# A hybrid decoder step: one key block of prompt attention turned later, and the input projection's row scaling moved from VectorE to ScalarE

## The reference

```python
hn = rms_norm(x, norm_mix)            # x * rsqrt(mean(x*x) + eps) * w
q_down, kv_down, qkv, z, b_raw, a_raw, gm, gg = jnp.split(hn @ w_in, IN_SPLITS, axis=-1)
```

```python
s = (einsum('bqhn,bkhn->bhqk', qn, k_nope) + einsum('bqhr,bkr->bhqk', qr, k_rope)) * MLA_SCALE
p = jax.nn.softmax(jnp.where(key_pos <= q_pos, s, NEG_BIG), axis=-1)
o = einsum('bhqk,bkhv->bqhv', p, v)
```

## Time and profile before

| | |
|---|---|
| three timed runs | 2679.3, 2688.88, 2682.79 us; median 2682.79 |
| the profiled execution | 2689.15 us, its span 2687.4 us |
| mean granted clock of TensorE | 0.942 |
| TensorE busy | 2454.0 us, 91% of the span |
| VectorE, ScalarE, GpSimd busy | 44%, 32%, 25% |

### The profile page before, as it was taken

The page is one execution under the profiler, slowest core; times in us unless marked ns, Lnnn a source line. Parts: engine busy times, 40 slices in busy tenths (PEclk is TensorE's granted clock), DMA queues, the critical chain, the costliest instruction groups (busy, mean ns, idle before and its releaser), DMA issues. The chain is left out here.

```text
span 2687.4 us, 48090 instructions
## 1 busy us (share of the span) xinstructions
PE 2454.0 (91%) x19566; PEld 1923.9 (72%) x19566; DVE 1177.1 (44%) x2282; ACT 849.0 (32%) x1774; POOL 659.1 (25%) x705
## 2 busy tenths in 40 slices
PE   5999999999799999699999999799998969999992
PEld 4999999999698888446555555666653537888871
DVE  6366664332257676335555555344442441111115
ACT  3257751141123233224444445243430111111112
POOL 0320000011244545143233230344420121101003
PEclk9999999999789999799999999799998979999996
DMA  4482233334443532400000000566646027998985
GB/s 137 135 262 69 92 102 104 114 123 139 131 121 94 145 113 71 149 6 25 25 25 25 25 25 9 219 229 267 254 170 214 32 78 285 326 324 321 321 288 214
DMA packets 184201, 390.22 MB, mean 145 GB/s; under 512 B 35488, under 2 KB 127044, under 8 KB 163117
## 3 DMA queue, kind: packets, MB, share of 16 engines
q1 hardware_dynamic: 148509, 236.82, 26.7%
q0 software_dynamic: 35504, 150.71, 15.4%
HBM read 306.54 MB, written 89.85 MB: 148 GB/s over the span
## 5 line engine op out<-in xcount | busy, mean ns | idle before, releaser
L136 PE MATMUL pi_acc<-hT_hi,pi_w_hi 128*128 128x352 f32 (+1 forms) x1152 | 378.4, 328 | 0.0
L136 PE MATMUL pi_acc<-hT_lo,pi_w_hi 128*128 128x352 f32 (+1 forms) x1152 | 371.3, 322 | 0.0
L136 PE MATMUL pi_acc<-hT_hi,pi_w_lo 128*128 128x352 f32 (+1 forms) x1152 | 371.3, 322 | 0.0
L136 PEld LDWEIGHTS pi_acc<-hT_hi,pi_w_hi 128*128 128x128 f32 x1152 | 217.2, 189 | 4.0 <-issue 3.8
L136 PEld LDWEIGHTS pi_acc<-hT_lo,pi_w_hi 128*128 128x128 f32 x1152 | 217.0, 188 | 4.0 <-issue 3.8
L136 PEld LDWEIGHTS pi_acc<-hT_hi,pi_w_lo 128*128 128x128 f32 x1152 | 216.9, 188 | 0.0
L1643 PE MATMUL at_sc<-at_keyT,at_qT 96*128 96x512 f32 (+5 forms) x480 | 161.3, 443 | 3.2 <-POOL at_qT L1573 2.3
L1895 ACT ACTIVATE at_p<-at_sc,at_nm 16x16 f32<-16x16 f32 (+5 forms) x144 | 100.7, 699 | 159.9 <-DVE at_nm L1758 158.6
L1756 DVE TENSOR_REDUCE at_mx<-at_sc 16x1 f32<-16x16 f32 (+5 forms) x144 | 101.4, 704 | 105.5 <-PE at_sc L1647 104.4
L2686 PEld LDWEIGHTS ex_gu<-ex_xT,wg 128*128 128x128 f32 x1056 | 133.0, 201 | 19.6 <-issue 19.6
L2411 PE MATMUL po_acc<-po_w,po_mix 128*128 128x512 f32 (+1 forms) x288 | 128.9, 602 | 10.3 <-DMA po_w<-w_out 10.3
(11 more groups left out here) (498 smaller groups left out, 4663.0 us busy)
## 6 DMA issues: line engine op xcount, KB each, us to landing
wg<-w_gate SPq DMA_DIRECT2D x33, 1024.0 KB, 6.3
wu<-w_up SPq DMA_DIRECT2D x33, 1024.0 KB, 8.6
wd<-w_down SPq DMA_DIRECT2D x33, 1024.0 KB, 8.3
pi_piece<-w_in SPq DMA_DIRECT2D x64, 384.0 KB, 3.6
expert_out<-pi_zero POOLq DMA_DIRECT2D x33, 512.0 KB, 12.1
expert_out<-ex_y SPq DMA_DIRECT2D x33, 512.0 KB, 8.5
projT<-pi_xr POOLq DMA_DIRECT2D x24, 524.0 KB, 3.2
convT<-pi_yn POOLq DMA_DIRECT2D x24, 512.0 KB, 2.9
```

The lines of the kernel that those rows point to most:

```text
L136: last = nc.tensor.matmul(out, lhs[a], rhs[b], start=(start and i == 0), stop=(stop and i == 2))
```

## The change

In prompt attention `turn` gets a second argument. `turn(u - 2, False)` stands where `turn` stood and turns the first two groups; `turn(u - 2, True)`, only for the last tile of a pair, turns the third group (the lone ninth block) behind the scores of unit `u` and the values of that round. ScalarE's copies keep their order.

In the input projection ScalarE does the scaling (a Copy activation with the root as its scale per row, at the end of the tile's square and root chain), and VectorE's list is put in a new order: `invert` (mean and reciprocal) runs one tile ahead, in round `t` come `invert(t + 1)` and `keep(t)`; the four pieces of job 0 follow round 0, and those of job 1 follow rounds 3 to 6, one each. ScalarE squares the next tile behind the scaling of this one. SyncE's and GpSimd's lists stay as they are.

```diff
-                def split_weights(job):
+                def split_weights(job, pieces=range(4)):
...
-                    for i in range(4):
+                    for i in pieces:
...
-                for t, (r0, n) in enumerate(TILES):
+                def invert(t):
+                    n = TILES[t][1]
                     dve.wait_ge(squared, t + 1)
                     nc.vector.tensor_scalar(mean[0:n, t:t + 1], ss[0:n, t:t + 1], 1.0 / D, EPS, ALU.mult, ALU.add).then_inc(meaned, 1)
                     dve.wait_ge(meaned, t + 1)
                     nc.vector.reciprocal(inv[0:n, t:t + 1], mean[0:n, t:t + 1]).then_inc(inverted, 1)
-                    dve.wait_ge(rooted, t + 1)
-                    if t >= 2:
-                        dve.wait_ge(turn_done, t - 1)
-                    nc.vector.tensor_scalar(xn[0:n, t % 2, :], x[0:n, t % 2, :], rstd[0:n, t:t + 1], None, ALU.mult).then_inc(scaled, 1)
-                    if t:
-                        keep(t - 1)
-                    if t == 1:
+
+                invert(0)
+                for t in range(NT):
+                    if t + 1 < NT:
+                        invert(t + 1)
+                    keep(t)
+                    if t == 0:
                         split_weights(0)
-                    if t == 5:
-                        split_weights(1)
-                keep(NT - 1)
+                    if 3 <= t < 7:
+                        split_weights(1, [t - 3])
...
-                for t, (r0, n) in enumerate(TILES):
+                def square_of(t):
+                    n = TILES[t][1]
                     act.wait_ge(x_loaded[t % 2], 16 * (t // 2 + 1) + (16 if t % 2 == 0 else 0))
...
+                def scale(t):
+                    n = TILES[t][1]
+                    act.wait_ge(rooted, t + 1)
+                    if t >= 2:
+                        act.wait_ge(turn_done, t - 1)
+                    nc.scalar.activation(xn[0:n, t % 2, :], x[0:n, t % 2, :], ACT.Copy, scale=rstd[0:n, t:t + 1]).then_inc(scaled, 1)
+
+                square_of(0)
+                for t in range(NT):
                     root(t)
+                    scale(t)
+                    if t + 1 < NT:
+                        square_of(t + 1)
                     if t:
                         keep_hi(t - 1)
...
-                def turn(u):
+                def turn(u, late):
                     n = shape(u)[3]
                     pe.wait_ge(normed, u + 1)
                     for g in range(first[u], first[u + 1]):
+                        if (g - first[u] == 2) != late:
+                            continue
...
                     if 2 <= u < U + 2:
-                        turn(u - 2)
+                        turn(u - 2, False)
...
                     if u >= 4 and u % 2 == 0:
                         values((u - 4) // 2)
+                    if 2 <= u < U + 2 and shape(u - 2)[1] == NT - 1:
+                        turn(u - 2, True)
```

## The result

The changed kernel takes 2638.33 us in the median of four runs (2636.5 to 2642.38), against 2681.51 for the kernel before, measured beside it. The ratio is 0.982, with a 95% interval of 0.9804 to 0.9835. Between the medians it is 43 us; 2636 us, 46.7 less, were forecast. The quotient of the two medians is 0.984, just above that interval, so by the ratio the gain is larger, 48 us; the result doesn't list the pairs that the ratio was made from. A second measurement on another occasion gave 2639.74 against 2690.86, ratio 0.9816 (0.9799 to 0.9833).

A forecast was written before the change was run, and what follows sets the result against it. TensorE, busy 91% of the span, was taken as the bound through its idle time and clock. Savings of 36.8 (attention) and 9.9 us (projection) sum to 46.7, giving 2636 us against the 2682.79 median; range 2628 to 2656.

The forecast's parts named there:

- Attention: Prompt attention's pair ends: covering the ninth block's wait saves 4.6 us at each of eight, 36.8 us in all.
- the values: Attention, pair end: the values run at full clock behind the next pair's scores and take 2.07 us.
- the end of a pair: Attention, first pair's end: from the eight turns at 1240.86, the next pair's projections start at 1246.1.
- rival B: Attention: the clock still falls at the pair boundary, only 2.2 us saved each, 2655 us in all; chance 0.10.
- Projection: Input projection: turns 5 to 7 come 5.12 us apart, 10.24 instead of 20.17 us, saving 9.9 us.
- the start: Input projection's start: two more scalings on ScalarE, one VectorE step less; -1 to +1.2 us, taken as 0.
- ScalarE's scaling: Input projection: scaling 128x1024 on ScalarE takes 1.06 us, bounds 0.75 and 1.06, hidden under TensorE's 5.12.
- VectorE's tile: Input projection: 3.4 us plus a 1.78 us piece, 5.2 against TensorE's 5.12; the 0.1 us lag per tile is hidden.
- C: Input projection: ScalarE or a piece is late, taking back 2.8 to 9.9 us; 2645 us; chance 0.06.
- D: Attention: the wait moves to head 1's ninth block, 2 us, and the clock falls there; 2673 us; chance 0.03.
- E: Attention: half clock lasts into the next pair's first projections, making the kernel slower, 2703 us with two stretches; chance 0.02.
- F: The new order changes nothing that is waited for, 2683 us; chance 0.03.

The follow-up runs named there:

- stall_filled: Kernel before plus 18 idle-time transposes ahead of the ninth block of head 0's last tile, order unchanged: 2669.91 us, ratio 0.9944.
- head_0_only: Only the attention change, against the kernel before, with head 0's ninth block late and head 1's left in line: 2656.49 us, ratio 0.9886.
- after_again: The changed kernel unaltered, measured a second time against the kernel before: 2639.74 us, ratio 0.9816.

## Why the prediction was right

- **Attention, 36.8 us forecast.** 37.4 in the profiled executions. By its steps: the values in 2.07 us, which is 32/36 of the 2.33 us that 36 of them took at a granted clock of 1.00 in the kernel before, measured 2.11; the ninth block without a wait, and there is none; the end of a pair in 5.24 (1246.1 - 1240.86), measured 5.20. That the clock stays up was the assumption that carried half of this; stall_filled shows that at a pair's end it hangs on TensorE standing (1.00 from 1188 to 1671 us with 18 transposes in each stall), and rival B didn't come (1.00 from 1176 to 1643 us). The prediction read at the first end that the fall comes while the stall is under 1 us old; over the eight ends of before it came 0.7 to 2.2 us after the stall began. Against the three other profiles with attention as before, the gain is 34 to 36: in those a fall at a pair's end lasted 3.4 us in one to three cases of eight, and 6.8 in the others. The before profile on which the sum rests had 6.8 at all eight, so the forecast took the upper end of what these profiles show.
- **Projection, 9.9 us forecast.** 9.5 at tile 8's turn, 9.7 over the tiles. Turns 5 to 7 came 10.12 us apart (44.40 to 54.52) and not 20.17, which is 10.05 saved; the start, taken as 0, lost 0.6 (tile 4's turn at 39.34, before at 38.77), inside its bounds.
- **The mis-sized term: ScalarE's scaling.** Taken as 1.06 us, the dearer end from the rows; it takes 1.15, outside the bounds that I had set:

```profile
45.76 1.15 ACT L690 ACTIVATE pi_yn<-pi_yn,pi_rstd 128x1024 f32<-128x1024 f32 x1
```

  ScalarE's Square of a tile of the same size takes 1.04 us in this profile (46.81). Why the scaling takes 0.11 more no run shows. On VectorE the same multiplication took 0.75 us; on the engine with time to spare (ScalarE is busy for 5.62 of 8 us in the window below) the dearer instruction was hidden all the same.
- **VectorE's tile, 5.2 us forecast against TensorE's 5.12.** It took less, and kept TensorE's pace, 5.06: piece 2 at 48.60, the next tile's mean at 50.20, the step that the next turn needs at 50.54:

```profile
48.60 0.47 DVE L129 TENSOR_SCALAR pi_m<-pi_piece 128x608 int32<-128x608 int32 x1
...
50.20 0.15 DVE L534 TENSOR_SCALAR pi_mean<-pi_ss 128x1 f32<-128x1 f32 x1
...
50.54 1.23 DVE L522 TENSOR_TENSOR pi_yn<-pi_extra,vecT 128x1024 f32<-128x1024 f32 x1
```

  That step ends at 51.8 and the turn that needs it starts at 54.52. But the window of these tiles (PE, PEld, DVE, ACT, POOL busy) shows VectorE busy for 7.76 of 8 us, 4.9 us of every 5.06: it has nearly become the bound.

```profile
49.00:57.00 8.00, 8.00 (x54) 7.94 (x53) 7.76 (x15) 5.62 (x9) 1.08 (x2) 1.00 0.54 138
```

- **What the sum left out.** The pieces' two slots: the block of the kernel before held a wait for a DMA too, 1.49 us ahead of its third piece, and with the pieces spread VectorE has no such wait:

```profile
50.62 0.48 DVE L129 TENSOR_SCALAR pi_m<-pi_piece 128x608 int32<-128x608 int32 x1 [1.49 <-DMA pi_piece<-w_in]
```

  It didn't change the sum, since that was made from TensorE's turns. Rivals C, D, E and F did not come; D was tried directly by head_0_only.
- **46.7 us forecast.** Between the medians it is 43, by the ratio 48 (44 to 53), in the second measurement 50 (45 to 54). By the lengths of the two stages it is 47, and 44 to 45 against the other three profiles with attention as before. The forecast lies among them. They differ by the spread of the runs (9.6 us between the four runs of before, 5.9 of after), much of it in the stage of the last section. That the median, 2638.33 us, lies only 2.3 from the forecast is closer than this spread warrants, and so far luck. From profile to profile the time fell by 52.7 us (2689.15 to 2636.5), of which 5.3 are the delta rule's, for which the sum has no term.

## What to carry to other kernels

Where an engine's list holds an instruction that must wait for another engine's copy, look down its list for work that doesn't need it: here 2 us of values were already there, and moving one line covered the wait. The stalls of 2 us on TensorE cost about twice their length here, because the granted clock behind them was 0.50 (some 17.5 us of wait and 17 to 20 of clock over eight stalls), so price the work behind a stall as well as the stall. And a block of side work on a feeding engine can be worth spreading even if its sum stays the same: here that alone took 7.1 us off the tiles, where the block's third piece had waited 1.49 us for its DMA and the spread pieces waited for none.

## What was not expected of the hardware

The delta rule's stage, untouched in all these kernels, took from 401.23 to 410.32 us, and goes with the time at half clock in it. Three kernels over that stage (windows; the granted clock is third from the right), before, after and the one with the slowest stage:

```profile
710.00:1118.00 408.00, 371.04 (x5882) 326.70 (x5882) 253.95 (x407) 122.28 (x181) 192.18 (x116) 0.91 0.40 113
```

```profile
701.00:1103.00 402.00, 366.07 (x5882) 321.41 (x5882) 253.05 (x407) 122.29 (x181) 192.27 (x116) 0.92 0.40 114
```

```profile
707.00:1118.00 411.00, 373.83 (x5884) 329.32 (x5884) 253.93 (x407) 122.28 (x181) 192.22 (x116) 0.90 0.40 112
```

0.91, 0.92 and 0.90 for 407.6, 402.3 and 410.3 us. By the clock's own records the stage holds 56.5 us at half clock in the shortest case (after_again) and 82.6 in the longest. Falls come there in some executions and not in others of the same kernel: after_again has one of 3.4 us at 961.8, where the first profile of the changed kernel has none. The stage is the largest part of the spread between the eleven profiles: 9.1 us, against 3.7 for all of the span outside the three columns (1681.2 to 1684.9 us). So it can hide changes of under some 8 us from the total, and a stage's own length in the profile is the better measure.

Not every fall there follows a stall. In the kernel before, TensorE was shown busy for all of 12 us ahead of the fall at 850.1:

```profile
838.00:850.00 12.00, 12.00 (x196) 11.33 (x194) 7.19 (x12) 3.30 (x7) 10.27 (x6) 1.00 0.69 210
850.10:853.50 3.40, 3.40 (x70) 3.40 (x68) 1.13 (x2) 0.36 (x1) 2.35 (x1) 0.50 0.00 0
```

So what the experiments show of stalls holds for the pairs' ends. Which of TensorE's work in this stage sets off a fall wasn't tried.
